# Gated delta rule: token-major gates, x's convolution ahead of the head pairs, beta on ScalarE, one sum of the second norm on VectorE

## The reference: what is computed

```python
qkv = silu(causal_dwconv(concat([q, k, v]), conv_w))
q = l2norm(q) * 128 ** -0.5; k = l2norm(k)
beta = sigmoid(b)
g = -exp(A_log) * softplus(a + dt_bias)            # a, b: 256 tokens x 8 heads
# in chunks of 64 tokens, per head
G = cumsum(g)
decay = exp(where(tril, G[:, None] - G[None, :], -inf))
L = where(strict, (k * beta) @ k.T * decay, 0)
u, w = solve(I + L, [v * beta, k * beta * exp(G)])
...
y_a = (bg * causal_dwconv(cg * xv, conv_a)) @ w_a_out     # the short convolution branch
y_b = gdn_branch(...) @ w_b_out
x = x + (sigmoid(ga) * y_a + sigmoid(gb) * y_b) @ w_o
x = x + conv_ffn(rmsnorm(x))
# second block starts with rmsnorm(x): x * rsqrt(mean(x * x) + EPS)
```

## Time and profile before

| | before |
|---|---|
| time of three runs, us | 1151.12, 1152.54, 1154.89; median 1152.54 |
| profiled execution, own time / span, us | 1156.57 / 1154.8 |
| mean granted TensorE clock | 0.995 of full |
| busy: PE, DVE, ACT, POOL | 98%, 67%, 52%, 18% |

### The profile page before, as it was taken

The page is one execution under the profiler, slowest core; times in us unless marked ns, Lnnn a source line. Parts: engine busy times, 40 slices in busy tenths (PEclk is TensorE's granted clock), DMA queues, the critical chain, the costliest instruction groups (busy, mean ns, idle before and its releaser), DMA issues. The chain is left out here.

```text
span 1154.8 us, 23245 instructions
## 1 busy us (share of the span) xinstructions
PE 1133.9 (98%) x10262; PEld 1104.9 (96%) x10262; DVE 769.7 (67%) x875; ACT 603.1 (52%) x692; POOL 205.9 (18%) x129
## 2 busy tenths in 40 slices
PE   9989899999999999999899999999999999999998
PEld 7989889999999999999899999999999999999998
DVE  6999775445456897796779757645666556756453
ACT  6978333242664765565655534433797335544341
POOL 0442364210133200000445400000011002211010
PEclk9999999999999999999999999999999999999999
DMA  8434333234365555555555553445444555555552
GB/s 304 152 137 150 119 111 106 81 111 135 121 224 201 194 185 187 208 191 186 179 178 182 168 187 126 142 146 183 151 144 172 190 184 183 183 188 208 189 188 105
DMA packets 27748, 192.81 MB, mean 167 GB/s; under 512 B 3072, under 2 KB 3200, under 8 KB 4992
## 3 DMA queue, kind: packets, MB, share of 16 engines
q1 hardware_dynamic: 27648, 191.33, 48.5%
HBM read 190.27 MB, written 1.05 MB: 166 GB/s over the span
## 5 line engine op out<-in xcount | busy, mean ns | idle before, releaser
L1236 DVE TENSOR_TENSOR wl<-raw,wh 128x2048 fp32r<-128x2048 f32 (+1 forms) x178 | 421.9, 2372 | 133.3 <-ACT wh L909 132.1
L909 ACT ACTIVATE wh<-raw 128x2048 fp32r<-128x2048 f32 x176 | 336.5, 1913 | 248.0 <-DMA raw<-in_wts 246.8
L566 PE MATMUL psS<-Yh,wh 128*128 128x256 f32 x1056 | 300.6, 285 | 1.5 <-issue 1.0
L566 PE MATMUL psS<-Yh,wl 128*128 128x256 f32 x1056 | 293.6, 278 | 0.0
L566 PE MATMUL psS<-Yl,wh 128*128 128x256 f32 x1056 | 293.5, 278 | 0.0
L566 PE MATMUL psS<-Xh,wh 128*128 128x256 f32 x896 | 260.2, 290 | 7.7 <-issue 6.7
L566 PE MATMUL psS<-Xl,wh 128*128 128x256 f32 x896 | 251.3, 280 | 0.0
L566 PE MATMUL psS<-Xh,wl 128*128 128x256 f32 x896 | 251.2, 280 | 0.0
L566 PEld LDWEIGHTS psS<-Yh,wh 128*128 128x128 f32 x1056 | 199.2, 189 | 4.7 <-issue 3.3
L566 PEld LDWEIGHTS psS<-Yl,wh 128*128 128x128 f32 x1056 | 198.8, 188 | 2.5 <-issue 1.9
L566 PEld LDWEIGHTS psS<-Yh,wl 128*128 128x128 f32 x1056 | 198.5, 188 | 0.0
(11 more groups left out here) (246 smaller groups left out, 2000.4 us busy)
## 6 DMA issues: line engine op xcount, KB each, us to landing
raw<-in_wts SPq DMA_DIRECT2D x176, 1024.0 KB, 4.8
raw<-in_wts SPq DMA_DIRECT2D x2, 512.0 KB, 6.1
gdn<-in_x SPq DMA_DIRECT2D x1, 1024.0 KB, 7.9
out<-head SPq DMA_DIRECT2D x4, 256.0 KB, 2.1
head<-in_x SPq DMA_DIRECT2D x1, 516.0 KB, 4.0
head<-in_x SPq DMA_DIRECT2D x1, 512.0 KB, 6.3
head<-in_sel SPq DMA_DIRECT2D x1, 512.0 KB, 3.9
xf<-in_dr SPq DMA_DIRECT2D x1, 512.0 KB, 5.7
```

The lines of the kernel that those rows point to most:

```text
L566: mm = pe.matmul(bank[:, half], a[:, n % SLOTS, p, :], b[:, kk_, :], start=(first and i == 0), stop=(last and i == 2), skip_group_check=True)
L909: act.activation(wh[:, n % SLOTS], raw[:, n % SLOTS], ACT.Copy).then_inc(sem["wh"], 1)
L1236: return dve.tensor_tensor(out, a, b, op)
```

## The change

Five edits, in words, and the diff.

1. Gates: PE transposes a and b right after their product (`ab_tok`, from block 7 to block 4), and the arithmetic is done on 128 partitions (tokens) with 16 values each, in `gw`; ACT's exponentials and logarithm stand around `l2n` at block 5, where its table is loaded anyway, instead of at 3 and 4 with loads of their own. `ab_cum` gets the row forms of G and beta by four matmuls of 40 rows instead of two of 8; ACT and DVE split them in two fp32r parts (`R`), and `rows` runs as two fp32r matmuls with 40 rows of contraction.
2. `gatec(j)` stands first in `TODO` of block x_j, on every engine, instead of last.
3. `VB` = v times beta is written by ACT, four instructions of 128x128 for a head pair, and not by DVE's third multiply.
4. The second norm's last addition to `ss[1]` is DVE's (`sum2(3)`), ahead of a weight split that was held back for later; POOL's fifth is left out there.
5. Buffers: `selr`, `R`, `gtok`, `gw` and the parameter columns follow.

```diff
@@ schedule
     put(3, "ab_mm")
-    put(4, "ab_gates")
-    put(5, "ab_decay")
-    put(7, "ab_tok")
+    put(4, "ab_tok")
+    todo[5].insert([step for step, a in todo[5]].index("l2n"), ("ab_exp", ()))
+    put(5, "ab_den")
+    todo[5].insert([step for step, a in todo[5]].index("l2n") + 2, ("ab_ln", ()))
+    put(6, "ab_decay")
     put(8, "ab_cum")
...
     for j in range(4):
         n = AT[("x", j)]
-        put(n, "gatec", j)
+        todo[n].insert(0, ("gatec", (j,)))
         put(n + 1, "mixc", j)
@@ PE
             def norm(i):
                 pe.wait_ge(sem["ss"], i + 1)
+                if i == 2:
+                    pe.wait_ge(sem["ssa"], 7)
...
             def ab_cum():
...
                 for t in range(2):
-                    mm = pe.matmul(psA[4][0:8, 1, t * P:(t + 1) * P], gtok[:, t, 0:8], tri, start=True, stop=True)
+                    pe.matmul(psA[4][0:40, 1, t * P:(t + 1) * P], gtok[:, 0, t, 0:40], tri, start=True, stop=True)
+                    mm = pe.matmul(psA[5][0:40, 0, t * P:(t + 1) * P], gtok[:, 1, t, 0:40], ident, start=True, stop=True)
                 mm.then_inc(sem["cum"], 1)
...
             def rows(h):
...
-                pe.matmul(psA[4 * (h % 2)][:, 0], sel[32:40, h], G2[32:40, :], start=True, stop=True)
-                pe.matmul(psA[4 * (h % 2) + 1][:, 1], sel[0:8, h], G3, start=True, stop=True).then_inc(sem["row"], 1)
+                pe.matmul(psA[4 * (h % 2)][:, 0], selr[:, h], R[:, 1], start=True, stop=True)
+                pe.matmul(psA[4 * (h % 2) + 1][:, 1], selr[:, h], R[:, 0], start=True, stop=True).then_inc(sem["row"], 1)
...
                 if b:
-                    pe.wait_ge(sem["tok"], 3 * b)
+                    pe.wait_ge(sem["tok"], 2 * b)
+                    pe.wait_ge(sem["vb"], 4 * b)
@@ ACT
-            def ab_mm():
+            def ab_exp():
                 exp_ln()
                 act.wait_ge(sem["abv"], 3)
...
             def ab_cum():
                 exp_ln()
+                act.wait_ge(sem["sel"], 16)
+                act.activation(selr[:], sel[0:40], ACT.Copy).then_inc(sem["selr"], 1)
+                act.wait_ge(sem["gs"], 1)
+                act.activation(R[:, 0], psA[4][0:40, 1], ACT.Copy).then_inc(sem["rh"], 1)
+                act.activation(R[:, 1], psA[5][0:40, 0], ACT.Copy).then_inc(sem["rh"], 1)
...
+            def tok(b):
+                act.wait_ge(sem["tk"], 2 * b + 2)
+                if b == 0:
+                    act.wait_ge(sem["tb"], 1)
+                for h in range(2):
+                    for t in range(2):
+                        act.activation(VB[:, 2 * b + h, t], psA[5][:, h, t * P:(t + 1) * P], ACT.Copy,
+                                       scale=TS[:, 1, 2 * b + h, t:t + 1]).then_inc(sem["vb"], 1)
@@ DVE
...
                 tt(KD[:, 2 * b:2 * b + 2], v, col(3), ALU.mult, "tok")
-                dve.wait_ge(sem["tk"], 2 * b + 2)
-                v = psA[5][:].rearrange("p a (c m) -> p a c m", m=P)
-                tt(VB[:, 2 * b:2 * b + 2], v, col(1), ALU.mult, "tok")
...
+            def sum2(j):
+                if j == 3:
+                    dve.wait_ge(sem["sqr"], 12)
+                    dve.wait_ge(sem["ssa"], 6)
+                    tt(ss[1][:], ss[1][:], t2[1][:], ALU.add, "ss")
@@ POOL
-                for g in range(per):
+                for g in range(per if j < 3 else 1):
```

More of the change, by code:

```diff
@@ L276 @@
 SEMS = """
-ab abT aba aqz abh abl abv abw am ao as at bag bs bst cum cv cx dec dr dt eg ev f1 f1h f2 f2h fp fq2 fs g2 g2z g3
+ab abT aba aqz abh abl abv abw am ao as at bag bs bst cum cv cx dec dr dt eg ev f1 f1h f2 f2h fp fq2 fs g2z g3
 gc gg gs gtok h h0 half hln hsum kb kk kn lt m2 m20 m2h ma mask mc md mm ms ms0 mx mx0 mxh nl nm nsum o oa oah oc
-og ogh on onr or orh out pa_ par pb_ pc pe pn pt qd qk r1 r2 r3 raw0 raw1 raw2 raw3 rawh rb rd res4 rg ri rl ro row rr rs rsp rt rtT
-rtk rtp ry s0 sc sel sg silu sp sq sqh sqp sqr sr ss ss0 ssa st t0 t0c tap tb tk tok tsa uw uwp vn warm wh wh0 wl wl0 xq ws x0 x0h
+og ogh on onr or orh out pa_ par pb_ pc pe pn pt qd qk r1 r2 r3 raw0 raw1 raw2 raw3 rawh rb rd res4 rh rg ri rl ro row rr rs rsp rt rtT
+rtk rtp ry s0 sc sel selr sg silu sp sq sqh sqp sqr sr ss ss0 ssa st t0 t0c tap tb tk tok tsa uw uwp vb vn warm wh wh0 wl wl0 xq ws x0 x0h
 x1 x1h x2 x3 x3h xT xTb xb xbh xres ya yah zp zs
@@ L323, in program @@
         with ExitStack() as own:
+            sb("under", [P, 6 * KT * S + 4 * S], F32, own)
+            selr = sb("selr", [40, H1, P], F32R, own)
+        with ExitStack() as own:
             Zh, Zl = sb("Zh", [P, KT, S], F32R, own), sb("Zl", [P, KT, S], F32R, own)
@@ L698, in left @@
                     pe.wait_ge(sem["t0c"], p + 1)
-                    pe.wait_ge(sem["tok"], 12)
+                    pe.wait_ge(sem["tok"], 8)
                 else:
@@ L1204, in _ @@
             steps = {"x0": x0, "norm": norm, "tap4": tap4, "gatec": gatec, "conv3": conv3, "silu": silu, "sig": sig,
-                     "zg": zg, "silur": silur, "gate1": gate1, "ffn1": ffn1, "l2n": l2n, "ab_mm": ab_mm, "ab_gates": ab_gates, "ab_cum": ab_cum,
-                     "rows": rows, "mixc": mixc, "lev0t": lev0t, "level": level, "uw": uw, "state": state, "o": o,
+                     "zg": zg, "silur": silur, "gate1": gate1, "ffn1": ffn1, "l2n": l2n, "ab_exp": ab_exp, "ab_ln": ab_ln, "ab_cum": ab_cum,
+                     "rows": rows, "mixc": mixc, "tok": tok, "lev0t": lev0t, "level": level, "uw": uw, "state": state, "o": o,
                      "onorm": onorm, "mix": mix, "res1": res1, "res2": res2, "sum2": sum2,
@@ L1393, in ab_decay @@
-            def ab_decay():
-                u, m, g = abt[0:8, 1], abt[0:8, 2], G2[0:8]
-                then(7, dve.tensor_tensor(g, g, den[0:8], ALU.mult))
-                then(8, dve.tensor_tensor(g, m, g, ALU.subtract))
-                then(9, dve.scalar_tensor_tensor(out=g, in0=u, scalar=0.0, in1=g, op0=ALU.max, op1=ALU.add))
-                dve.tensor_scalar(g, g, small[0:8, 8:9], -1.0, ALU.mult, ALU.mult).then_inc(sem["g2"], 1)
-            def ab_tok():
-                dve.wait_ge(sem["abT"], 1)
-                dve.tensor_copy(gtok[:], flat(4)[:, 0:80].rearrange("p (t c) -> p t c", t=2)).then_inc(sem["gtok"], 1)
+                tt(abt[:], psA[4][0:64, 0], rb[0:64], ALU.mult, "abv")
@@ new lines, in ab_tok, with ab_den @@
+            def ab_tok():
+                u, m = gw[:, 0], gw[:, 3]
+                bias = par[:, PAR["dt_b"]:PAR["dt_b"] + 8].unsqueeze(1).broadcast_to([P, 2, H1])
+                dve.wait_ge(sem["abT"], 1)
+                then(2, tt_(u, ab(0), bias, ALU.add))
+                stt(m, u, -1.0, u, ALU.mult, ALU.max, "abv")
+            def ab_den():
+                dve.wait_ge(sem["aba"], 3)
+                then(4, dve.tensor_scalar(gw[:, 4:6], gw[:, 1:3], 1.0, None, ALU.add))
+                stt(gw[:, 3], gw[:, 4], -1.0, gw[:, 1], ALU.add, ALU.subtract, "abv")
@@ new lines, in ab_decay, with both, over @@
+            def ab_decay():
+                u, m, d = gw[:, 0], gw[:, 3], gw[:, 4:6]
+                def both(k):
+                    return gtok[:, k].rearrange("p t (r c) -> p t r c", r=2)[:, :, :, 0:H1]
+                def over(v):
+                    return v.unsqueeze(2).broadcast_to([P, 2, 2, H1])
+                dve.wait_ge(sem["aba"], 4)
+                then(6, dve.reciprocal(d, d))
+                then(7, tt_(m, m, d[:, 0], ALU.mult))
+                then(8, tt_(m, gw[:, 1], m, ALU.subtract))
+                then(9, dve.scalar_tensor_tensor(out=m, in0=u, scalar=0.0, in1=m, op0=ALU.max, op1=ALU.add))
+                rate = small[:, 8:16].unsqueeze(1).broadcast_to([P, 2, H1])
+                then(10, dve.scalar_tensor_tensor(out=m, in0=m, scalar=-1.0, in1=rate, op0=ALU.mult, op1=ALU.mult))
+                dve.wait_ge(sem["g2z"], 1)
+                dve.tensor_copy(both(0), over(m)).then_inc(sem["gtok"], 1)
+                dve.tensor_copy(both(1), over(d[:, 1])).then_inc(sem["gtok"], 1)
@@ L1753, in add_squares @@
                     return
-                for g in range(per):
+                for g in range(per if j < 3 else 1):
                     pool.wait_ge(sem["sqr"], done + per * j + g + 1)
                     src = (sq, t2)[g][j % 2][:]
-                    last = j == 3 and g == per - 1
-                    name = "ss" if last else "ssa"
+                    name = "ss" if j == 3 and i != 2 else "ssa"
                     if j > 1:
```

66 lines of the change are left out of this document (29 added, 37 removed).

## The result

The changed kernel takes 1164.62 us (median of four, 1163.91 to 1167.39) against 1152.32 us (median of four): 12.3 us more. The ratio of its runs to those of before is 1.009, 95% interval 1.0049 to 1.0132. Slower was forecast, with 1158 and a range up to 1162; the time lies 2.6 us outside it, and the loss is over twice the forecast one.

What follows compares the result with a forecast made beforehand. PE, at work 98% of the span, was taken as the bound, so its idle and low-clock time count. Terms summed to +6.0 on the 1152.54 us median, 1158.5, stated as 1158; forecast range 1156 to 1160.5, overall 1151 to 1162.

Steps and rivals of the forecast that it cites:

- the three new stalls: Before pair 2's transposes and the first products of levels 0 and 3: PE idles 3 to 4.5 us each.
- Gates, -4.7 +0.4: Block 8's stall and its low clock vanish, -4.7 us; more and taller matmuls in `ab_cum` add 0.4.
- Rows, -0.7 a block: Blocks 10 to 13's steps: two 40-row fp32r passes per head replace fp32 pairs, -0.7 us a block, -2.8 in all.
- the +0.9 a block that was weighed: `rows` passes: if serial passes cost twice a pair's time, the edit adds 0.9 us a block.
- What the head pairs give back, 6.2: From `rows(2)` to block 15: PE arrives early and waits, 2.0 us for ACT's exponential, then smaller waits; +6.2 in all.
- First convolution, -3.3: x0, block 16: stall and low clock vanish, -5.0 us; a wait for the last `kk`'s mask adds 1.7.
- Second, +5.7: x1: pair 2's transposes wait 4.2 us for `tok(1)` behind the convolution, with 1.5 of low clock; +5.7 us.
- Third restart, -3.7: Before pair 3's transposes: the wait of 2.0 us and 1.7 of low clock vanish, -3.7 us.
- Levels, +5.1 each: Levels 0 and 3: masks behind POOL's product stall PE some 3.6 us, plus 1.5 of low clock; +5.1 us each.
- the rival in which it takes 1.28 there: x1, x2, x3: POOL's product wins the ports from DVE's split, shortening the stalls; faster, 1148 us; chance 0.14.
- the cancelling rival: x1: convolution avoids POOL's masks, takes 1.67 us instead of 4.84; gains and losses cancel, +1.0, 1153.5 us; chance 0.22.
- Norm, -2.0: Second norm: DVE's last addition lets PE start sums 2.5 us sooner, `rb` only about 1.0 sooner; taken as -2.0 us.

Runs made afterwards that it cites:

- the version with the sum: The changed kernel with gatec first only at x0 and last at x1, x2 and x3, the norm's sum still on DVE; 1150.45 us, 0.997 of before.

## Why the prediction was wrong in size

The direction, the three new stalls, their places, releasers and lengths were right, and so was what the first convolution and the norm's sum win. The sum was 6.0, of which 5.5 was forecast. The steps of the table that it priced add to +8.2, the rest of PE's work to another +2.9, and the medians lie 12.3 apart.

The mechanism was right, and what failed is sizes. Three terms were mis-sized: the cheaper `rows` passes (-0.7 a block, measured -0.4, 1.2 us in all), the low clock taken as 1.5 behind every stall (it was more at level 0, where +5.1 became +6.1), and the third restart, priced from one execution (-3.7, measured -2.9). That is 3.0 us, of which other terms, above all the first convolution, gave back 0.8. The larger part of the miss, 4.1 us, is no term's: 2.9 in blocks that the prediction took as unchanged, most of it different from one execution to the next, and 1.2 between profiles and medians. The priced steps alone, at +8.2, would have given 1160.5. Point by point.

**Gates, -4.7 +0.4.** Right: -4.9 at block 8 and some +0.6 at blocks 9 and 10 for `ab_cum`. The small instructions were not uniformly small, though. Alone they take 0.17 to 0.34 us, but GpSimd was at work from 47.93 to 50.29 and from 53.70 to 57.91:

```profile
49.31 0.17 DVE L1263 TENSOR_TENSOR gw<-psP,par 128x16 f32<-128x16 f32 x1
49.51 0.81 DVE L1269 SCALAR_TENSOR_TENSOR gw<-gw 128x16 f32<-128x16 f32 x1
...
55.41 1.29 DVE L1415 TENSOR_SCALAR gw<-gw 128x32 f32<-128x32 f32 x1
56.73 1.20 DVE L1269 SCALAR_TENSOR_TENSOR gw<-gw 128x16 f32<-128x16 f32 x1
```

Of 16 values on each partition, an instruction took 0.17, 0.81 or 1.20 us, more than the 0.6 that was set as the bound from above. The excess was hidden here.

**Rows, -0.7 a block.** Too much. The four passes of block 11:

```profile
88.59 0.38 PE L661 MATMUL psP<-R,selr 40*128 40x256 f32 x1
88.81 0.28 PE L662 MATMUL psP<-R,selr 40*128 40x256 f32 x1
88.93 0.28 PE L661 MATMUL psP<-R,selr 40*128 40x256 f32 x1
89.05 0.28 PE L662 MATMUL psP<-R,selr 40*128 40x256 f32 x1
```

They start 0.12 to 0.22 apart, and the next weight matmul at 89.25, so 0.66 us in place of about 1.0; block 11 took 6.43 us in both profiles of the change and 6.83 in all three of before. So each block won 0.4 and not 0.7, and the four together 1.2 less than forecast. The argument from the Trainium skill (TensorEngine Tiling (Array Packing), Available Configurations) was incomplete, since the page also lists row tiles of 64, into which 40 rows would fit. Its conclusion came true all the same: none of the four passes starts beside another. They are cheap without it, and the +0.9 a block that was weighed didn't come.

**What the head pairs give back, 6.2.** Right in total, wrong in kind. PE reached `rows(2)` when it was said to, but it waited 2.41 and not 2.0, since ACT's exponential came 0.89 sooner (96.96 for 97.85) and not 1.6. Behind it the clock fell to 0.50, which the prediction had not reckoned, and block 12 cost +4.5 and not +1.3. The smaller waits that followed took 1.5 in all instead of 4.2. Idle time of 3.9 us in blocks 12 to 15 and 1.7 lost to the clock make 5.6. The low clock took the place of later waits and didn't add to them: the run without the norm's sum kept full clock at `rows(2)`, waited at `rows(6)` and `rows(7)` instead, and needed 34.13 us for blocks 12 to 15; the version with the sum needed 34.11 with the low clock. The other profiles with this chain and x0's convolution in front lost 1.7 or 3.4 us to the clock there and needed 34.1 to 34.3. The chain through ACT sets the pace here: with 1.06 us of ACT's copy taken out of it the wait was 0.76 shorter and the four blocks took 33.4. To the end of block 15, without the late start of the profiles, the changed kernel stood at +0.2 where -0.9 was said.

**First convolution, -3.3.** Right, -3.9. **Second, +5.7.** Right, +5.6, with POOL's product 3.27, the convolution 4.81 and 3.52 of idle. **Third restart, -3.7.** Too much: that was one execution's price. Over three it is -2.9, and the one at 0.97 us would give about -1.1.

**Levels, +5.1 each.** +6.1 and +5.2: the waits are 3.56 and 3.62 as worked out, and the slow stretch behind costs more at level 0, where the granted clock was 0.50 throughout. At x1, x2 and x3 POOL's product took 3.24 to 3.27 us, so the rival in which it takes 1.28 there never came near. The run with the product on VectorE shows that the product was the cause. Its convolution did take 1.65 us, as the cancelling rival said, but only after that.

**`VB`, no term.** Pair 3's transposes don't wait in the changed kernel, so nothing shows there. With the convolution first at x0 only, the one profile without this edit waited 1.07 us longer at that place.

**Norm, -2.0.** Right, -2.1, with some luck: 0.6 of it is the low clock in the third profile of before, and VectorE's addition took 1.70 us and not 0.7. The sum of squares was ready 0.28 after PE asked, and `rb` let block 83 wait 1.75.

**What no term had.** Two stretches differ in every profile with the gates' edit: blocks 33 to 48 take 1.8 us more, without any idle time, and blocks 84 to 98 take 1.3 less. Together that is only +0.4; what in the edit or its buffers does it wasn't tested. The rest varies between executions of one kernel. One of the two profiles of the change lost 1.1 us in block 4, where PE idled for 0.88, and it began 0.4 later, so block 7 ends 1.1 later in the mean. And the last 78 blocks took 476.4 us in one and 473.5 in the other, which makes +1.2 in the mean; among all eleven profiles with the gates' edit six took 476.2 to 476.4 and five 473.4 or 473.5. The spacing of the weight matmuls, 0.113 or 0.118 us, makes these differences. Nothing in the rows of before spoke of it, though windows of before at both spacings were there to be compared (91 and 87 matmuls in 10 us at full clock). What sets it isn't settled. Some 1.2 more lies between the profiles' means (+11.1) and the medians (+12.3), which is within the interval.

**And the discount.** The prediction took 1158 for 1158.5, on the ground that slack in a queue shortens a wait. The waits at pair 2 were 0.7 shorter, but the discount was small beside what was missing. With one case it can't be said whether such sums come out too small as a rule.

## What to carry to other kernels

When work is moved to the front of several queues at once, ask at each engine what now stands behind it. Here the same move took 4 us off block 16 at x0, and cost 17 at three other places through one 1.3 us product on GpSimd that takes 3.3 beside a long two-input VectorE instruction; moved to VectorE, where it took 0.7 to 1.3, it freed all three. A gain of idle time early in the kernel is kept only if the engine that feeds the next step is early too: 5 us won at block 8 were given back in blocks 12 to 15. Reckon with a slow stretch behind each new wait as long as those that had one, but don't add it where further waits for the same engine follow: there it can take their place, as it did here. And take a stall's size from more than one execution.
